# Down weights of the expert steps issued by ScalarE instead of SyncE

## The chip, the core and the metric

The kernel runs on one core of one Trainium2 chip. The metric is the device time of one execution in microseconds (us). A core has TensorE (matmuls), VectorE, ScalarE, GpSimd and SyncE, each with an instruction stream of its own, tied together by semaphores, and 16 DMA engines that all of them share.

## The reference

One layer of a decoder trunk in float32, for 1024 prompt tokens and 8 sample tokens (1032 rows of width 1024): RMSNorm, one input projection, four token mixers side by side (RWKV-7, causal pooling, a Conformer convolution, Mamba-2), gates, an output projection and a residual. Then a mixture of experts, which is the part that matters here, and a last RMSNorm:

```python
x = x + m                                    # m: the token mixers
x = x + hier_moe(rmsnorm(x, norm_ffn_g), lw) # 16 experts, hidden width 256, 2 of them for each token
...
hg = jnp.einsum('bld,edf->blef', h, moe_w_gate[e]); hu = jnp.einsum('bld,edf->blef', h, moe_w_up[e])
act = jax.nn.silu(hg) * hu * gate[..., e, None]
out = out + jnp.einsum('blef,efd->bld', act, moe_w_down[e])
```

Each token goes to one group of four experts and to the best two in it.

## The kernel before

All up to the router (about 1290 us) is not touched. The expert stage follows. The pairs of token and expert are sorted by expert and cut into slots of 32 rows that belong to one expert each. There are 80 slots, in 20 steps (`STEPS`) of four (`NS = 4`): in step i, slot j works on rows 32j to 32j+31 of the arrays with the weights of its expert, in `GU[j]` and `DN[j]`. Slot j of step i is slot 20j + i of the sorted list, so each j passes through the experts in order, and its expert mostly stays the same from one step to the next.

A table in memory, `exps`, holds for each step and slot the expert's number and a flag that says whether it differs from that of the step before. It is written once (`routed` reaches 3). The engine that issues a load reads the eight numbers of a step into registers (`look_up`), and each load has `cond=f`: with the flag at 0 nothing is moved, and the semaphore still counts up. Only the down weights of step 0 have no condition. The gate/up weights of four guessed experts (`GUESS`) are fetched before the router is through, and step 0 replaces those that were guessed wrong.

Sizes: the gate/up weights of an expert are 2 MB. They come in four pieces (`GUC = 4`, 128 rows of 4 KB, 0.5 MB each), each with its semaphore `gu_in{h}`. The down weights are 1 MB (128 rows of 8 KB), semaphore `dn_in`. Both are held once per slot number: piece h of step i+1 can be fetched only when `gu_mm{h}` says that step i has used it, and the down weights when `dn_mm0` and `dn_mm1` say so (the two halves of the output columns). Both halves read the same buffer.

TensorE's order, from line 1064:

```python
turn_rows(0); turn_rows(1); gate_up(0)
for i in range(STEPS):
    if i + 2 < STEPS: turn_rows(i + 2)      # turns the gathered rows XG, L1024
    turn_act(i)                             # L1033
    if i + 1 < STEPS: gate_up(i + 1)        # 64 matmuls, 16 for each piece, L1045
    down(i)                                 # 32 matmuls, waits for dn_in, L1059
```

`gate_up(i)` waits for the four pieces one after the other. SyncE issues all weights in one queue: for step 0 the pieces, then the down weights; then, for each i, the four pieces of step i+2, each behind its wait for `gu_mm{h}` (L473 and L475), and the down weights of step i+1 behind the waits for `dn_mm0` and `dn_mm1` (L508 to L510, issued at L486; those of step 0 at L483). ScalarE copies the turned rows (`rows_turned`, L1361), takes the Silu (`gated`, L1368) and copies the first half of the output (`downed`, L1375). VectorE multiplies (L2005), copies the turned activations (L2012) and the second half (L2018). GpSimd gathers the input rows two steps ahead (L2228, 0.5 MB a step, from a queue of its own) and scatters the output rows (L2234).

Of the kernel before, what the change touches and what calls it, by code (L numbers as in the profile page):

```python
# [13 lines left out]
P = 128  # L14
# [16 lines left out]
NE = 16  # L31
# [21 lines left out]
NS = 4  # L53
# [3 lines left out]
STEPS = (NSLOTS + NS - 1) // NS  # L57
# [85 lines left out]
def build(nc, ins, outs):  # L143
    ctx = ExitStack()
    with ctx:
# [5 lines left out]
        def sem(name):  # L151
            if name not in sems:
                sems[name] = ctx.enter_context(nc.semaphore(name))
            return sems[name]
# [41 lines left out]
        exps = ctx.enter_context(nc.sbuf_tensor("exps", [P, STEPS, 2, NS], I32))  # L196
# [172 lines left out]
        DN = [arena[:, 2 * D * j:2 * D * (j + 1)] for j in range(NS)]  # L369
# [18 lines left out]
        def _(sp):  # L388
# [70 lines left out]
            guess_gu(3)  # L459

            gu_e = ins["w_gu"].rearrange("(e p) f -> p e f", p=P)
            dn_e = ins["w_dn"].rearrange("(e p) f -> p e f", p=P)
            regs = [[ctx.enter_context(sp.register(f"slot_{s}_{q}")) for q in range(2 * NS)] for s in range(2)]

            def look_up(i):

                sp.load(regs[i % 2], exps[0:1, i:i + 1, :, :].rearrange("p a b c -> p (a b c)"))

            def load_gu(i, h):

                w = GUW // GUC
                for j in range(NS):
                    e = sp.snap(regs[i % 2][j], donate=False, min_val=0, max_val=NE - 1)  # L473
                    f = sp.snap(regs[i % 2][NS + j], donate=False, min_val=0, max_val=1)
                    sp.dma_start(GU[j][:, h * w:(h + 1) * w].unsqueeze(1), gu_e[:, bass.ds(e, 1), h * w:(h + 1) * w], cond=f  # L475
                                 ).then_inc(sem(f"gu_in{h}"), 16)

            def load_dn(i):

                for j in range(NS):  # L480
                    e = sp.snap(regs[i % 2][j], donate=False, min_val=0, max_val=NE - 1)
                    if i == 0:
                        sp.dma_start(DN[j].unsqueeze(1), dn_e[:, bass.ds(e, 1), :]).then_inc(sem("dn_in"), 16)  # L483
                    else:
                        f = sp.snap(regs[i % 2][NS + j], donate=False, min_val=0, max_val=1)
                        sp.dma_start(DN[j].unsqueeze(1), dn_e[:, bass.ds(e, 1), :], cond=f).then_inc(sem("dn_in"), 16)  # L486

            sp.wait_ge(sem("h2_out0"), 16 * 5)
            sp.wait_ge(sem("h2_out1"), 16 * 4)
            sp.wait_ge(sem("routed"), 3)  # L490
# [3 lines left out]
            sp.wait_ge(sem("xg_in0"), 16)  # L494
            for h in range(GUC):
                load_gu(0, h)
            load_dn(0)
            look_up(1)
            for h in range(GUC):
                sp.wait_ge(sem(f"gu_mm{h}"), NS)  # L500
                load_gu(1, h)
            for i in range(STEPS - 1):
                if i + 2 < STEPS:
                    look_up(i + 2)
                    for h in range(GUC):
                        sp.wait_ge(sem(f"gu_mm{h}"), NS * (i + 2))
                        load_gu(i + 2, h)
                sp.wait_ge(sem("dn_mm0"), NS * (i + 1))  # L508
                sp.wait_ge(sem("dn_mm1"), NS * (i + 1))
                load_dn(i + 1)  # L510

            sp.wait_ge(sem(f"gu_mm{GUC - 1}"), NS * STEPS)
            sp.wait_ge(sem("dn_mm1"), NS * STEPS)
# [576 lines left out]
        def _(act):  # L1090
# [42 lines left out]
            for n in range(4):  # L1133
                act.wait_ge(sem("lora_mm"), n + 1)
                dst, b = ((SG, "w0"), (AA, "a0"))[n // 2]
# [220 lines left out]
            def rows_turned(i):  # L1356

                act.wait_ge(sem("xt_mm"), i + 1)
                if i >= 2:
                    act.wait_ge(sem(f"gu_mm{GUC - 1}"), NS * (i - 1))  # L1360
                A(XT[i % 2], ps[:, 2:4, :].rearrange("p a b -> p (a b)"), ACT.Copy).then_inc(sem("xt_ev"), 1)  # L1361

            def gated(i):

                act.wait_ge(sem(f"gu_mm{GUC - 1}"), NS * (i + 1))
                if i:
                    act.wait_ge(sem("act"), i)
                A(SIL, ps[:, i % 2, 0:HID], ACT.Silu).then_inc(sem("silu"), 1)  # L1368

            def downed(i):  # L1370

                act.wait_ge(sem("dn_mm0"), NS * (i + 1))
                if i >= 2:
                    act.wait_ge(sem(f"yo_out{i % 2}"), 16 * (i // 2))
                A(YO[i % 2][:, 0:HALF], ps[:, 5, :], ACT.Copy).then_inc(sem("yo_ev0"), 1)  # L1375

            rows_turned(0)
            rows_turned(1)
            gated(0)
            for i in range(STEPS):  # L1380
                if i + 2 < STEPS:
                    rows_turned(i + 2)
                if i + 1 < STEPS:
                    gated(i + 1)
                downed(i)
            act.wait_ge(sem("xt_mm"), STEPS)
            for b, n in enumerate(ON_PE):
                for c in range(2):
# [981 lines left out]
```

## Time and profile before

| | |
|---|---|
| time before, median of 3 runs | 1639.51 us (1638.74 to 1641.35) |
| the profiled execution, its own time | 1640.04 us |
| its span, first to last instruction | 1638.2 us |
| granted TensorE clock over the span | 0.976 |
| TensorE busy with matmuls | 1523.8 us, 93% |
| expert stage, first gate/up matmul to last down matmul | about 1307.6 to 1589.7 us |

All rows below are of the profiled execution. Times at the start of a row are microseconds from the start of the span. "SPq" is SyncE issuing a DMA; "idle before <- releaser" is how long the engine stood still and what ended it. "issue" as a releaser means that the profile shows nothing that it waited for. Queue q1 is the hardware queue of SyncE, q0 that of GpSimd.

### The profile page before, as it was taken

What the parts mean: (1) busy time and instruction counts of PE and PEld (TensorE: products, weight loads), DVE (VectorE), ACT (ScalarE), POOL (GpSimd) and SP (SyncE); (2) the same over time, 40 slices, a digit from 0 to 9 for tenths busy, and PEclk for the clock granted to TensorE, in tenths of its full rate; (3) what the DMA queues carried; (4) which work ended last, traced back from release to release, by engine and by line L of the source; (5) the groups of instructions that cost most, each with busy time, mean ns of one, the idle gap of its engine ahead of it and who ended that gap; (6) DMA issues with size and microseconds to landing.
All of it is one profiled execution on the core that took longest, in us unless ns stands there. A gap on an engine that the chain in (4) does not pass through costs nothing.

```text
span 1638.2 us, 20753 instructions
## 1 busy us (share of the span) xinstructions
PE 1523.8 (93%) x8005; PEld 984.3 (60%) x8005; DVE 741.3 (45%) x1394; ACT 341.7 (21%) x633; POOL 205.6 (13%) x316
## 2 busy tenths in 40 slices
PE   8999999999999999999999999999999397978965
PEld 5888666577777777777777765666444232322312
DVE  5655199842534344636344323577844401101116
ACT  3001311412213131331313145000121211111113
POOL 3008300012111101101010010000000001101100
PEclk9999999999999999999999999999999699989997
DMA  7101011033221312111103120465200878675647
GB/s 218 52 26 52 18 40 35 30 121 102 64 71 52 111 42 73 49 56 52 48 35 125 48 106 32 174 274 180 110 39 26 292 262 327 245 263 207 224 171 301
DMA packets 47235, 194.70 MB, mean 119 GB/s; under 512 B 6408, under 2 KB 6904, under 8 KB 42400
## 3 DMA queue, kind: packets, MB, share of 16 engines
q1 hardware_dynamic: 28144, 116.13, 20.0%
q0 software_dynamic: 18992, 77.25, 13.2%
q8 instruction: 63, 1.03, 0.3%
q14 instruction: 36, 0.29, 0.1%
HBM read 353.23 MB, written 41.44 MB: 241 GB/s over the span
## 4 chain that ended last, share of the span: by engine, by line
PE 84%; DMA 6%; DVE 4%; issue 2%; SPq 2%; ACT 2%; POOL 0%; DVEq 0%; POOLq 0%; ACTq 0%
PE ps L548 29%; PE ps L616 7%; PE ps L896 7%; PE ps L945 6%; PE ps L1045 6%; PE ps L1059 3%; PE ps L840 3%; DMA arena<-in_w_gu 3%; PE ps L754 2%; PE ps L749 2%; PE ps L759 2%; PE ps L732 2%; SPq L475 1%; PE ps L563 1%; DMA scr<-h_rows,idx 1%
## 5 line engine op out<-in xcount | busy, mean ns | idle before, releaser
L548 PE MATMUL ps<-arena,wring 128*128 128x344 f32 x1728 | 528.5, 452 | 0.6 <-DVE arena L1471 0.6
L548 PEld LDWEIGHTS ps<-arena,wring 128*128 128x128 f32 x1728 | 314.4, 189 | 143.6 <-issue 1.9
L1045 PE MATMUL ps<-arena,scr 128*32 128x512 f32 x1280 | 150.4, 617 | 20.3 <-DMA arena<-in_w_gu 19.9
L2117 POOL DMA_DIRECT2D gate_scratch<-stage x96 | 52.1, 544 | 618.6 <-ACT stage L1185 542.8
L896 PE MATMUL ps<-arena,wring 128*128 128x344 f32 x384 | 111.2, 451 | 0.0
L1045 PEld LDWEIGHTS ps<-arena,scr 128*32 128x32 f32 x1280 | 39.3, 112 | 115.8 <-issue 83.7
L896 PEld LDWEIGHTS ps<-arena,wring 128*128 128x128 f32 x384 | 72.5, 189 | 38.6
L1185 ACT ACTIVATE stage<-ps 128x344 f32<-128x344 f32 x84 | 38.4, 457 | 252.8 <-PE ps L548 252.7
L2005 DVE TENSOR_TENSOR scr<-scr,ps 128x256 f32<-128x256 f32 x20 | 8.4, 421 | 181.4 <-ACT scr L1368 181.4
L1059 PE MATMUL ps<-arena,scr 128*32 128x512 f32 x640 | 76.1, 617 | 15.3 <-issue 13.9
L1702 DVE TENSOR_TENSOR scr<-scr,ps 128x512 f32<-128x512 f32 x40 | 27.5, 688 | 127.9 <-PE ps L754 127.9
L1576 DVE SCALAR_TENSOR_TENSOR arena<-arena,vec 128x1024 f32<-128x1024 f32 x60 | 74.4, 1282 | 1.1
L616 PE MATMUL ps<-scr,arena 128*128 128x258 f32 x288 | 64.3, 381 | 0.0
L840 PE MATMUL ps<-arena,wring 128*128 128x344 f32 x192 | 59.3, 470 | 3.3 <-ACT stage L1159 3.3
L1059 PEld LDWEIGHTS ps<-arena,scr 128*32 128x32 f32 x640 | 22.0, 114 | 67.0 <-issue 65.4
L616 PEld LDWEIGHTS ps<-scr,arena 128*128 128x128 f32 x288 | 54.6, 190 | 8.0
L945 PE MATMUL ps<-arena,scr 128*128 128x512 f32 x128 | 58.2, 599 | 0.0
L1471 DVE TENSOR_TENSOR arena<-arena,ps 128x258 f32<-128x258 f32 x70 | 27.9, 421 | 58.5 <-PE ps L616 58.2
L840 PEld LDWEIGHTS ps<-arena,wring 128*128 128x128 f32 x192 | 37.6, 197 | 24.6 <-ACT stage L1159 3.9
L1225 ACT ACTIVATE scr<-ps 128x512 f32<-128x512 f32 x40 | 23.9, 597 | 130.4 <-PE ps L749 130.4
L2234 POOL DMA_INDIRECT y_rows<-scr,idx x20 | 19.6, 978 | 243.7 <-DVE scr L2018 239.0
L749 PEld LDWEIGHTS ps<-scr 128*128 128x128 f32 x320 | 41.9, 191 | 8.0
(450 smaller groups left out, 2091.8 us busy)
## 6 DMA issues: line engine op xcount, KB each, us to landing
arena<-in_w_gu SPq DMA_DIRECT2D x336, 512.0 KB
arena<-in_w_dn SPq DMA_DIRECT2D x80, 1024.0 KB
wring<-in_w_all SPq DMA_DIRECT2D x55, 512.0 KB, 3.6
gate_scratch<-stage POOLq DMA_DIRECT2D x96, 172.0 KB, 2.2
arena<-gate_scratch POOLq DMA_DIRECT2D x4, 2064.0 KB, 10.5
scr<-gate_scratch POOLq DMA_DIRECT2D x4, 2064.0 KB, 10.4
arena<-y_rows SPq DMA_DIRECT2D x16, 512.0 KB, 9.6
arena<-in_w_out SPq DMA_DIRECT2D x2, 2048.0 KB, 15.7
```

Source lines behind the costliest of these rows:

```text
L548: mm = pe.matmul(ps[:, c, 0:CW], wring[:, slot, k, :], H[:, k, chunk(c)], start=k == 0, stop=k == KT - 1)
L616: mm = pe.matmul(ps[:, g % 6, 0:QT], left[k][:, j, :], src[:, j, c], start=j == 0, stop=j == 3)
L732: mm = pe.matmul(ps[:, 4 + n, (q % 2) * 256:(q % 2) * 256 + 256], (BT if n < 2 else KTB)[:, q, :], KR[:, q, :, :].rearrange("p a b -> p (a ...
L749: mm = pe.matmul(ps[:, 6, q * P:(q + 1) * P], NLB[:, q, :], U[:, q, :], start=True, stop=True)
L840: mm = pe.matmul(ps[:, 6 + m % 2, 0:CW], wring[:, n % 2, k, :], H[:, k, chunk(c)], start=k == 0, stop=k == KT - 1)
L896: mm = pe.matmul(ps[:, m % 6, 0:CW], wring[:, n % 2, 2 * b + k, :], row(2 * b + k, c * CW, (c + 1) * CW), start=k == 0, stop=k == 1)
L945: mm = pe.matmul(ps[:, bank, :], left[:, k, :], right[:, k, :], start=k == 0, stop=k == 3)
L1045: mm = pe.matmul(ps[S * j:S * (j + 1), i % 2, :], XT[i % 2][:, k * P + S * j:k * P + S * (j + 1)], GU[j][:, k * 2 * HID:(k + 1) * 2 * HID] ...
L1059: mm = pe.matmul(ps[S * j:S * (j + 1), 5 + h, :], ATB[:, k, S * j:S * (j + 1)], DN[j][:, k * D + h * HALF:k * D + (h + 1) * HALF], start=k ...
L1185: A(stage[:, c, :], ps[:, c, 0:CW], ACT.Sigmoid).then_inc(sem("evac"), 1)
L1576: ins_ = ts(dst, src, w, v("conv_b", t), MUL, ADD) if j == 0 else stt(dst, src, w, dst, MUL, ADD)
L2117: pool.dma_start(gate_scratch[:, g:g + 1, chunk(c)], stage[:, c:c + 1, :]).then_inc(sem(f"gate_out{c}"), 16)
```

## The change

The down weights of every step are issued by ScalarE. It has eight registers of its own and loads them from `exps` at each step. For step 0 it does so ahead of its first work in the stage, as soon as the table is there and the first gather has landed; for step i+1 behind the copy of the first half of step i and a wait for `dn_mm1`. SyncE keeps the pieces of gate/up and its own look-ups.

```diff
@@ SyncE
-            def load_dn(i):
-                for j in range(NS):
-                    e = sp.snap(regs[i % 2][j], ...)
-                    if i == 0:
-                        sp.dma_start(DN[j].unsqueeze(1), dn_e[:, bass.ds(e, 1), :]).then_inc(sem("dn_in"), 16)
-                    else:
-                        f = sp.snap(regs[i % 2][NS + j], ...)
-                        sp.dma_start(DN[j].unsqueeze(1), dn_e[:, bass.ds(e, 1), :], cond=f).then_inc(sem("dn_in"), 16)
...
             for h in range(GUC):
                 load_gu(0, h)
-            load_dn(0)
             look_up(1)
...
                         load_gu(i + 2, h)
-                sp.wait_ge(sem("dn_mm0"), NS * (i + 1))
-                sp.wait_ge(sem("dn_mm1"), NS * (i + 1))
-                load_dn(i + 1)
@@ ScalarE
+            regs = [ctx.enter_context(act.register(f"down_{q}")) for q in range(2 * NS)]
+            def load_dn(i):
+                act.load(regs, exps[0:1, i:i + 1, :, :].rearrange("p a b c -> p (a b c)"))
+                for j in range(NS):
...                 # the same snaps and DMAs, by act
+            act.wait_ge(sem("routed"), 3)
+            act.wait_ge(sem("xg_in0"), 16)
+            load_dn(0)
             rows_turned(0)
             rows_turned(1)
             gated(0)
             for i in range(STEPS):
                 if i + 2 < STEPS:
                     rows_turned(i + 2)
                 if i + 1 < STEPS:
                     gated(i + 1)
                 downed(i)
+                if i + 1 < STEPS:
+                    act.wait_ge(sem("dn_mm1"), NS * (i + 1))
+                    load_dn(i + 1)
```

## Rows read from the trace of the kernel before

**Rows 1.** The page, busy time of each engine and its share of the span.

```profile
PE 1523.8 (93%) x8005; PEld 984.3 (60%) x8005; DVE 741.3 (45%) x1394; ACT 341.7 (21%) x633; POOL 205.6 (13%) x316
```

**Rows 2.** Waits, 1290 to 1600: total us, times, longest.

```profile
PE ps L1045 <- DMA arena<-in_w_gu: 19.9, 9, 4.9
PE ps L1059 <- issue: 13.9, 5, 5.1
```

**Rows 3.** Timeline of TensorE: last piece of gate_up(4), and down(3).

```profile
1365.88 1.92 PE L1045 MATMUL ps<-arena,scr 128*32 128x512 f32 x16 [3.62 <-DMA arena<-in_w_gu]
1369.63 3.64 PE L1059 MATMUL ps<-arena,scr 128*32 128x512 f32 x32 [1.82 <-issue]
```

**Rows 4.** Timeline of TensorE: down(4), (9), (13), turn_rows(16), down(18).

```profile
1384.60 5.32 PE L1059 MATMUL ps<-arena,scr 128*32 128x512 f32 x32 [3.09 <-issue]
...
1460.29 5.03 PE L1059 MATMUL ps<-arena,scr 128*32 128x512 f32 x32 [5.08 <-issue]
...
1516.76 3.64 PE L1059 MATMUL ps<-arena,scr 128*32 128x512 f32 x32 [1.35 <-issue]
1520.87 1.09 PE L1024 MATMUL ps<-cst,scr 128*128 128x128 f32 x8 [0.47 <-DMA scr<-h_rows,idx]
...
1580.55 3.64 PE L1059 MATMUL ps<-arena,scr 128*32 128x512 f32 x32 [2.57 <-issue]
```

**Rows 5.** Waits of SyncE, 1250 to 1638: total us, times, longest.

```profile
SPq L509 <- PE ps L1059: 43.2, 15, 11.4
```

**Rows 6.** Timeline of SyncE's issues: gu(0), dn(0), dn(3), dn(4), gu(6), gu(11), dn(13), gu(15).

```profile
1302.89 7.85 SPq L475 DMA_DIRECT2D arena<-in_w_gu  x16
...
1310.95 1.98 SPq L483 DMA_DIRECT2D arena<-in_w_dn  x4
...
1356.04 1.56 SPq L486 DMA_DIRECT2D arena<-in_w_dn  x4
...
1373.70 1.78 SPq L486 DMA_DIRECT2D arena<-in_w_dn  x4
1376.77 8.20 SPq L475 DMA_DIRECT2D arena<-in_w_gu  x16
...
1450.47 6.84 SPq L475 DMA_DIRECT2D arena<-in_w_gu  x16
...
1507.63 1.79 SPq L486 DMA_DIRECT2D arena<-in_w_dn  x4
1510.67 8.14 SPq L475 DMA_DIRECT2D arena<-in_w_gu  x16
```

**Rows 7.** Lines L467 (register loads) and L475: ns min/median/max.

```profile
L467 SPq TENSOR_LOAD <-exps x20: 361/524/727, 1289.9 to 1558.9; - x20
...
L475 SPq DMA_DIRECT2D arena<-in_w_gu x320: 2/73/352, 1302.9 to 1569.0; - x160
```

**Rows 8.** DMA queues, 1433 to 1435: packets, MB, share of 16 engines.

```profile
q1 hardware_dynamic: 116, 0.42, 51.5%
q0 software_dynamic: 117, 0.41, 50.6%
```

**Rows 9.** DMA queues, 1454 to 1457, q1 with down weights.

```profile
q1 hardware_dynamic: 115, 0.81, 64.4%
q0 software_dynamic: 116, 0.47, 38.1%
```

**Rows 10.** Timeline of TensorE: gate_up(0), matmuls and one of their weight loads.

```profile
1312.60 7.05 PE L1045 MATMUL ps<-arena,scr 128*32 128x512 f32 x48 [2.12 <-DMA arena<-in_w_gu]
1317.33 0.13 PEld L1045 LDWEIGHTS ps<-arena,scr 128*32 128x32 f32 x4 [0.30 <-DMA arena<-in_w_gu]
```

**Rows 11.** Timeline of GpSimd: the gather of step 3.

```profile
1307.93 0.94 POOL L2228 DMA_INDIRECT scr<-h_rows,idx  x1 [1.73 <-PE ps L1024]
```

**Rows 12.** Busy time in 1384.5 to 1388: engines, then granted clock, DMA share, GB/s.

```profile
1384.50:1388.00 3.50, 3.40 (x17) 1.00 (x21) 0.00 (x0) 0.00 (x0) 0.00 (x0) 0.52 1.03 418
```

More of the change, by code:

```diff
@@ L461, in _ @@
             gu_e = ins["w_gu"].rearrange("(e p) f -> p e f", p=P)
-            dn_e = ins["w_dn"].rearrange("(e p) f -> p e f", p=P)
             regs = [[ctx.enter_context(sp.register(f"slot_{s}_{q}")) for q in range(2 * NS)] for s in range(2)]
@@ L476, in load_gu @@
                                  ).then_inc(sem(f"gu_in{h}"), 16)
-            def load_dn(i):
-                for j in range(NS):
-                    e = sp.snap(regs[i % 2][j], donate=False, min_val=0, max_val=NE - 1)
-                    if i == 0:
-                        sp.dma_start(DN[j].unsqueeze(1), dn_e[:, bass.ds(e, 1), :]).then_inc(sem("dn_in"), 16)
-                    else:
-                        f = sp.snap(regs[i % 2][NS + j], donate=False, min_val=0, max_val=1)
-                        sp.dma_start(DN[j].unsqueeze(1), dn_e[:, bass.ds(e, 1), :], cond=f).then_inc(sem("dn_in"), 16)
             sp.wait_ge(sem("h2_out0"), 16 * 5)
@@ L1375, in downed @@
                 A(YO[i % 2][:, 0:HALF], ps[:, 5, :], ACT.Copy).then_inc(sem("yo_ev0"), 1)
+            dn_e = ins["w_dn"].rearrange("(e p) f -> p e f", p=P)
+            regs = [ctx.enter_context(act.register(f"down_{q}")) for q in range(2 * NS)]
+            def load_dn(i):
+                act.load(regs, exps[0:1, i:i + 1, :, :].rearrange("p a b c -> p (a b c)"))
+                for j in range(NS):
+                    e = act.snap(regs[j], donate=False, min_val=0, max_val=NE - 1)
+                    if i == 0:
+                        act.dma_start(DN[j].unsqueeze(1), dn_e[:, bass.ds(e, 1), :]).then_inc(sem("dn_in"), 16)
+                    else:
+                        f = act.snap(regs[NS + j], donate=False, min_val=0, max_val=1)
+                        act.dma_start(DN[j].unsqueeze(1), dn_e[:, bass.ds(e, 1), :], cond=f).then_inc(sem("dn_in"), 16)
+            act.wait_ge(sem("routed"), 3)
+            act.wait_ge(sem("xg_in0"), 16)
+            load_dn(0)
             rows_turned(0)
```

## The prediction

> **What bounds the kernel now.** I read the page first: TensorE is busy for 93% of the span [rows 1], so only its idle time can be won or made. Then the waits of the expert stage (about 1303 to 1590 us). TensorE is stopped there in two ways: 19.9 us before gate/up matmuls until a piece of weights lands, and 13.9 us before down matmuls, five times, which the profile calls "issue" [rows 2]. In those five places nothing but `dn_in` is missing, so I read them as waits for down weights. Next, where they are: gate_up(4) stops 3.62 us for its last piece, then down(3) 1.82 us [rows 3]; down(4), down(9), down(13) and down(18) stop 3.09, 5.08, 1.35 and 2.57 us [rows 4]. The other steps show no stop of this kind.
>
> Is SyncE what is late? It sat 43.2 us waiting for TensorE's down matmuls [rows 5], and its order follows TensorE's: the pieces of step i+2 go out during gate_up(i+1), the down weights of step i+1 after down(i), and the next piece can be issued only when gate_up(i+2) has used its buffer. The first piece goes out 2 to 3 us after the last down issue (1373.70 + 1.78 to 1376.77, 1507.63 + 1.79 to 1510.67) [rows 6]. So a down issue holds up no later piece that could have gone. What is short in the stalls is transfer time. A transfer whose expert stays the same is skipped; its issue takes 0.073 us, one that runs 0.34 [rows 7].
>
> **The look-up and issue on ScalarE.** Removed from SyncE: four issues a step. Added to ScalarE: a register load (0.524 us median on SyncE) [rows 7] and the same four issues, 1.2 to 2.0 us [rows 6]. ScalarE comes here after the copy of the first half of down(i) and waits for the second half, which TensorE ends about when it did for SyncE. The look-up now stands behind that wait, so each down transfer starts some 0.5 us later. Behind it on ScalarE stands the copy of the turned rows (needed a step later) and the Silu (due after a 7 us gate_up). In the steady step they hide the 2.5 to 3 us. The 0.5 us shows only where down already waits for its weights: down(4), (9), (13), (18): 4 x 0.5 = +2.0. Bounds: 0, if the register load is fetched faster than SyncE's, to +3.2 at 0.8 each.
>
> **What two hardware queues do to the order.** Until now down weights of step i+1 stand in one queue behind the pieces of step i+2 that TensorE needs first, and ahead of those of step i+3. From now on they are in a queue of their own. The trace has a second queue already, POOL's gathers and scatters, and shows how two queues share. Where both carry 4 KB rows they moved 116 and 117 packets, 0.42 and 0.41 MB [rows 8]. Where the hardware queue carries down weights (8 KB rows), it was 115 and 116 packets, but 0.81 against 0.47 MB, in 3 us: 427 GB/s, with shares that add up to all 16 engines [rows 9]. So queues take turns by packet, and a down transfer gets two bytes for each byte of gate/up. At 427 GB/s an engine needs 0.154 us for 4 KB and 0.307 for 8 KB. A transfer is 128 rows, 8 for each engine. A turn is thus 0.46 us with down and one other queue busy, and 0.61 with all three.
>
> The Trainium skill (DMA: Bandwidth & Descriptors, Issuing engines are not separate DMA queues) says that transfers issued by different engines run on the same 16 DMA engines and interleave, so that only the sequencer's issue time is saved. The trace agrees with the first half: 0.81 and 0.47 MB in 3 us out of a full set of engines [rows 9].
>
> **Step 0, dn(0) against gu(0).** Before, dn(0), 4 MB, was issued at 1310.95, after all pieces of gu(0) (1302.89 to 1310.7) [rows 6]. One of the four guessed experts is reloaded, so each piece is one transfer of 0.5 MB; the first goes out at about 1303.7 and moves from about 1304.8 (estimates from the row). gate_up(0) ran its last 48 matmuls from 1312.60, the last piece landed at 1317.33, and it ended at 1319.65 [rows 10]. Now ScalarE issues dn(0) from about 1303.2, as soon as the first gather lands, and its 32 rows per engine are there with the first piece. Piece 0: 8 turns of 0.46 = 3.7 us, to 1308.5. POOL's gathers (2) and (3), 16 rows an engine, come in from about 1308 [rows 11]. Pieces 1 and 2: 8 turns of 0.61 = 4.9 us each, to 1318.3; the gathers are then done. Piece 3: 3.7 us, to 1322.0, plus about 1.2 us to the semaphore (estimate from dn(9), whose full engines end a little before down(9) starts): 1323.2. Its 16 matmuls take 1.92 [rows 3]: gate_up(0) ends at 1325.1 instead of 1319.65. **+5.5.** dn(0) is landed long before down(0) then, which wins nothing, since down(0) did not stop before. Lower bound: if the queues shared bytes evenly, the pieces would land some 2 us late, +1.9. Upper bound: the matmuls run at the low clock after these idle stretches, +7.5. ScalarE also turns XT(0) some 1 us later, which lies under the wait for piece 1 (2.12 us) [rows 10]. I take 5.5, as the packet counts say.
>
> **dn(3) against gu(4).** dn(3), one expert, was issued at 1356.04 [rows 6] behind pieces of gu(4) that were still moving. Now it passes them. The same bytes are moved by the same time, when dn(3) landed (1369.6), but the last to land is piece 3 of gu(4), not dn(3). Behind it still lie 1.92 us of matmuls: down(3) starts at 1371.5 instead of 1369.63 [rows 3]. **+1.9.** Below: 0, if piece 3 kept its turn; it can't be a gain over 1.8, the wait itself. The idle stretch before piece 3 grows from 3.6 to 4.9 us. After the 3.09 us before down(4) the granted clock was 0.52 [rows 12] (the 1.2 GHz level) and the product took 5.32 instead of 3.64 [rows 4, 3]. After 3.62 us in gate_up(4) it had not fallen. For 4.9 us I count such a fall: **+1.7** (0 to 1.7).
>
> **dn(4) against gu(6), dn(13) against gu(15).** dn(4), two experts, was issued at 1373.70 and gu(6) behind it at 1376.77; dn(13) at 1507.63 and gu(15) at 1510.67 [rows 6]. Each had SyncE's queue to itself until it was through. Now a third queue takes turns from some 2 us after the first down row. dn(4) then has about 10 of its 16 rows per engine left; with POOL also busy each costs 0.61 instead of 0.46: 8 to 10 x 0.15 = 1.2 to 1.5, and about two of them share with gate/up alone at 0.46 instead of 0.31: +0.3. **+1.7 for down(4), +1.5 for down(13)**, whose last rows met POOL's later. Its wait is followed by one of 0.47 for a gather [rows 4], which the shift takes in: -0.4. Bounds: 0 to 2.5 each. dn(9) and dn(18) have no gate/up transfers beside them (gu(11) is all skipped, 16 issues in 6.84 us [rows 6], and there is no step 20): only the 0.5 us.
>
> **Sum.** 2.0 + 5.5 + 1.9 + 1.7 + 1.7 + 1.5 - 0.4 = 13.9 us. The stops of gate_up(9), (13) and (18) stay, as dn(8), dn(12) and dn(17) are skipped. Nothing takes the sum back: steps 5 to 8, 10 to 12 and 14 to 17 are bound by TensorE and are only shifted. The profiled execution took 1640.0 (span 1638.2): 1653.9, which is 1653.4 against the median of 1639.5, since that lies 0.5 below.
>
> **The rivals.**
> 1. The forecast, 1653.4, chance 0.48.
> 2. The clock falls in every new idle stretch: also in gate_up(0) (+1.9), before down(13), whose stop grows from 1.35 to over 3 us (+1.7), and down(18), 2.57 to 3.1 us (+1.7). For it speaks down(4) with 3.09 us [rows 4], against it gate_up(4) with 3.62 at full clock [rows 3]. 1639.5 + 13.9 + 5.3 = 1658.7. Chance 0.17.
> 3. The hardware queues share bytes evenly, or a piece passes between large rows: 1.9 for step 0, 1.9 for dn(3), 1.0 for each of dn(4) and dn(13), 2.0 for the look-up, no clock: +7.8 - 0.4, 1646.9. Against it stand the packet counts of [rows 9], but these are of POOL's queue, not of a second hardware one. Chance 0.20.
> 4. Nothing measurable: SyncE's small pieces find their turn at once, and only look-ups show: +2.0, 1641.5. Chance 0.08. This needs spare engines, and in the stalls they are full.
> 5. Faster, by one mechanism: the stops before down come from standing behind gate/up in one queue. With its own, dn(3) lands some 5 us sooner and the 1.82 us are gone; dn(4) is issued sooner too, and if the engines gave both queues more together, its 3.09 would shrink. At -1.8 - 3.1 it gives 1634.6. It decides once passing costs piece 3 of gu(4) less than 1.8 us; the full engines speak against it. Chance 0.04.
>
> **How the numbers follow.** A measurement of this kernel tells 0.2%, 3.3 us, from no change. The range takes in cases 1 and 3 and most of 2: 1644.5 to 1661; what is left out are 4, 5 and a little of 2 and 3, under 2 in 10. Rivals 1 to 3 are slower by over 0.2% (0.85, less a little of 3), rival 4 and that little make "same" 0.10, rival 5 faster 0.04; the 0.03 left goes to slower, for costs that I have not seen. Slower 0.86, same 0.10, faster 0.04.
>
> **What would show it.** In the profile after: gate_up(0)'s last piece lands at about 1323 and the matmuls of L1045 wait several times in step 0; down(3) follows gate_up(4) without a stop, and gate_up(4) stops over 6 us; the stops before down(4) and down(13) are 2 us longer; those before down(9) and down(18) 0.5. In the waits, the total of L1045 for its weights rises from 19.9 to about 28, that of L1059 from 13.9 to about 17. If gate_up(0) ends before 1321.6, the sharing by packets is wrong; if down(3) starts before 1369.6, passing costs nothing. A wait of TensorE for ScalarE anywhere (for a copy of turned rows that stands behind the new issues) would be a cost that I have at zero.

## The result, and the profile after

The changed kernel takes 1659.6 us, median of 5 (1657.1 to 1661.6), against 1641.0 us (1638.7 to 1641.5) for the kernel before on the same chip: ratio 1.0112, interval 1.0093 to 1.0130, +18.6 us. I had forecast 1653.4, range 1644.5 to 1661: the sign held, the size was 6 us short. The change cost 18.6 us where my sum had 13.9; the rest is that the kernel before has a median of 1641.0 here and had 1639.5 in its first three runs.

In the changed kernel L474 is SyncE's gate/up issue, L1371 and L1374 ScalarE's down issues, L1367 its look-up, L1030 the matmuls of gate_up, L1044 those of down (L1045 and L1059 before), L1009 and L1346 the turning of rows and ScalarE's copy of them. First the page: TensorE's busy time, then each hardware queue, then the down issues.

```profile
PE 1531.1 (92%) x8005; PEld 986.9 (60%) x8005; DVE 741.2 (45%) x1394; ACT 341.6 (21%) x633; POOL 205.6 (12%) x316
...
q1 hardware_dynamic: 25552, 97.25, 17.0%
q10 hardware_dynamic: 2592, 18.88, 3.2%
...
arena<-in_w_dn ACTq DMA_DIRECT2D x80, 1024.0 KB
```

TensorE runs the same 8005 matmuls, but 7.3 us longer than in [rows 1]: some of them run at a lower clock. q10 is ScalarE's new queue, with all of the down weights. Now the waits of the expert stage (total us, times, longest).

```profile
PE ps L1030 <- DMA arena<-in_w_gu: 24.1, 12, 5.3
...
PE ps L1044 <- issue: 19.6, 5, 6.9
...
PE ps L1009 <- ACT scr L1346: 6.0, 1, 6.0
```

and in the kernel before, the line that answers to the third:

```profile
PE ps L1024 <- ACT scr L1361: 1.2, 1, 1.2
```

The first two answer to [rows 2]: +4.2 and +5.7 us. The five stops ahead of down are not the same five: that of down(3) is gone, and one ahead of down(19) has come. The third has grown by 4.8 us: TensorE waits once for ScalarE's copy. The timeline of ScalarE and then of TensorE shows where:

```profile
1306.96 5.51 ACTq L1371 DMA_DIRECT2D arena<-in_w_dn  x4
1312.52 1.02 ACT L1346 ACTIVATE scr<-ps 128x1024 f32<-128x1024 f32 x1 [26.16 <-issue]
```

```profile
1313.68 1.94 PE L1009 MATMUL ps<-cst,scr 128*128 128x128 f32 x8 [5.97 <-ACT scr L1346]
1315.56 5.51 PE L1030 MATMUL ps<-arena,scr 128*32 128x512 f32 x32
1323.46 1.92 PE L1030 MATMUL ps<-arena,scr 128*32 128x512 f32 x16 [2.39 <-DMA arena<-in_w_gu]
1327.92 1.92 PE L1030 MATMUL ps<-arena,scr 128*32 128x512 f32 x16 [2.54 <-DMA arena<-in_w_gu]
...
1370.37 1.92 PE L1030 MATMUL ps<-arena,scr 128*32 128x512 f32 x16 [0.45 <-DMA arena<-in_w_gu]
1377.58 3.50 PE L1030 MATMUL ps<-arena,scr 128*32 128x512 f32 x16 [5.29 <-DMA arena<-in_w_gu]
1380.91 3.61 PE L1044 MATMUL ps<-arena,scr 128*32 128x512 f32 x32
...
1397.76 5.34 PE L1044 MATMUL ps<-arena,scr 128*32 128x512 f32 x32 [5.00 <-issue]
...
1475.51 5.75 PE L1044 MATMUL ps<-arena,scr 128*32 128x512 f32 x32 [6.93 <-issue]
...
1534.50 5.26 PE L1044 MATMUL ps<-arena,scr 128*32 128x512 f32 x32 [2.93 <-issue]
...
1598.79 5.34 PE L1044 MATMUL ps<-arena,scr 128*32 128x512 f32 x32 [2.89 <-issue]
```

The first block is step 0: the turning of the second rows waits 5.97 us (1.21 before) while ScalarE issues dn(0), and then gate_up(0) still stops twice for pieces. The second is gate_up(4) and down(3): the old 1.82 us ahead of down(3) [rows 3] are gone, and the last 16 matmuls of gate_up(4) took 3.50 instead of 1.92. The last four are down(4), (9), (13) and (18), to be held against [rows 4].

To place the rest, I count from the first gather of the stage, because what lies ahead of it is untouched by the edit and differed by 3.2 us between the two profiles (1298.22 and 1301.45; in a second profile of the kernel before it was 1299.83, and over all fourteen profiles of this document it lies between 1298.2 and 1303.4, with kernels in which ScalarE issues down weights at both ends). This is how late the changed kernel is, against the kernel before, at the end of each down product:

| end of | before | after | late by |
|---|---|---|---|
| down(0) | 33.4 | 40.3 | 6.9 |
| down(3) | 75.1 | 83.1 | 8.0 |
| down(4) | 91.7 | 101.6 | 9.9 |
| down(9) | 167.1 | 179.8 | 12.7 |
| down(13) | 222.2 | 238.3 | 16.1 |
| down(18) | 286.0 | 302.7 | 16.7 |
| down(19) | 291.4 | 308.6 | 17.2 |

So step 0 costs 6.9, the passing of gu(4) 1.1, and 8.7 lies at the four stops: these are 5.6 us longer and the products behind them 4.1, of which about 1 us is made up, most of it in gate_up(18). By my sum it had been 5.5, 3.6 and 4.8. The last 0.5 us comes at down(19), which stops longer than in the kernel before (the second line):

```profile
1606.38 3.64 PE L1044 MATMUL ps<-arena,scr 128*32 128x512 f32 x32 [1.88 <-issue]
```

```profile
1585.94 3.64 PE L1059 MATMUL ps<-arena,scr 128*32 128x512 f32 x32 [1.38 <-DVE scr L2012]
```

Nothing is moved for step 19, but its semaphore counts up only with the four skipped issues, and the last of them ends 0.06 us ahead of down(19) here and 0.07 before, where the profile names VectorE. They too stand behind the late look-up; my sum had this at nothing.

The queues in 1320 to 1323 (packets, MB, share of 16 engines), with all three at work:

```profile
q10 hardware_dynamic: 88, 0.61, 48.5%
q0 software_dynamic: 79, 0.32, 26.2%
q1 hardware_dynamic: 83, 0.32, 25.9%
```

Near-equal packets and nearly twice the bytes for the 8 KB rows: turns by packet hold for a second hardware queue as for GpSimd's in [rows 9]. The Trainium skill (DMA: Bandwidth & Descriptors, Queues, rings and completion order) says that an engine goes round its queues at the boundaries of packets. A packet there is a group, some 9 to 17 descriptors as a rule; a packet of these rows is one row of weights. The trace agrees that the turns are even (88, 79 and 83); how many rows make one turn these counts do not show.

### The profile page after: what moved, and what is told of

Read it like the earlier page. It is cut to its first block, busy times and chain, and to the rows that moved or that the text cites. A ratio compares the mean times of both kernels' runs of the same rounds, so it can differ in the third digit from the quotient of the medians.

```text
span 1658.2 us, 20757 instructions
## 1 busy us (share of the span) xinstructions
PE 1531.1 (92%) x8005; PEld 986.9 (60%) x8005; DVE 741.2 (45%) x1394; ACT 341.6 (21%) x633; POOL 205.6 (12%) x316
## 4 chain that ended last, share of the span: by engine, by line
PE 84%; DMA 6%; DVE 4%; issue 3%; SPq 2%; ACT 2%; POOL 0%; DVEq 0%; POOLq 0%; ACTq 0%
PE ps L533 29%; PE ps L601 7%; PE ps L881 7%; PE ps L930 6%; PE ps L1030 6%; PE ps L1044 4%; DMA arena<-in_w_gu 4%; PE ps L825 3%; PE ps L734 2%; PE ps L739 2%; PE ps L717 2%; PE ps L744 2%; SPq L474 1%; PE ps L548 1%; PE ps L1009 1%
## 5 line engine op out<-in xcount | busy, mean ns | idle before, releaser
L1030 PE MATMUL ps<-arena,scr 128*32 128x512 f32 x1280 | 150.7, 617 | 24.2 <-DMA arena<-in_w_gu 24.1
L1030 PEld LDWEIGHTS ps<-arena,scr 128*32 128x32 f32 x1280 | 39.1, 112 | 119.9 <-issue 82.2
L1044 PE MATMUL ps<-arena,scr 128*32 128x512 f32 x640 | 80.6, 648 | 19.6 <-issue 19.6
L1044 PEld LDWEIGHTS ps<-arena,scr 128*32 128x32 f32 x640 | 22.9, 119 | 75.2 <-issue 75.2
L2239 POOL DMA_INDIRECT y_rows<-scr,idx x20 | 19.6, 979 | 256.1 <-DVE scr L2023 250.9
L2023 DVE COPY scr<-ps 128x512 f32<-128x512 f32 x20 | 13.8, 692 | 80.8 <-PE ps L1044 80.8
```

The source lines that it names most:

```text
L1030: mm = pe.matmul(ps[S * j:S * (j + 1), i % 2, :], XT[i % 2][:, k * P + S * j:k * P + S * (j + 1)], GU[j][:, k * 2 * HID:(k + 1) * 2 * HID] ...
L1044: mm = pe.matmul(ps[S * j:S * (j + 1), 5 + h, :], ATB[:, k, S * j:S * (j + 1)], DN[j][:, k * D + h * HALF:k * D + (h + 1) * HALF], start=k ...
```

## The experiments

Ratios are against the kernel before on the same chip; us are the ratio times 1640. "Stops" are those ahead of down(4), (9), (13), (18) in the profile; "down(0)" and "down(19)" are their ends after the first gather, and "profiled" is the profiled execution's time less the median of its kernel, in us.

| kernel | ratio (interval) | us | profiled | down(0) | stops | sum | down(19) |
|---|---|---|---|---|---|---|---|
| before | | | | 33.4 | 3.1, 5.1, 1.3, 2.6 | 12.1 | 291.4 |
| before, again | 0.9999 (0.9984 to 1.0014) | 0 | -0.8 | 32.8 | 2.9, 4.7, 1.3, 2.2 | 11.1 | 289.5 |
| changed kernel | 1.0112 (1.0093 to 1.0130) | +18.4 | +0.4 | 40.3 | 5.0, 6.9, 2.9, 2.9 | 17.7 | 308.6 |
| dn(0) on SyncE | 1.0062 (1.0045 to 1.0079) | +10.2 | -2.0 | 32.8 | 5.6, 6.0, 2.9, 3.5 | 17.9 | 295.7 |
| only dn(0) moved | 1.0057 (1.0035 to 1.0078) | +9.3 | -5.1 | 40.0 | 2.8, 5.5, 1.4, 2.4 | 12.0 | 292.6 |
| early small DMA | 1.0139 (1.0114 to 1.0164) | +22.8 | +1.2 | 42.1 | 5.4, 6.9, 3.6, 2.9 | 18.7 | 312.5 |
| dn(0) after the turns | 1.0066 (1.0046 to 1.0087) | +10.8 | +0.4 | 34.1 | 5.3, 7.3, 2.8, 3.1 | 18.6 | 299.7 |
| look-up ahead | 1.0059 (1.0037 to 1.0081) | +9.7 | +1.6 | 40.3 | 3.1, 5.5, 1.7, 2.2 | 12.5 | 301.3 |
| gate/up behind down | 1.0124 (1.0101 to 1.0146) | +20.3 | -1.1 | 40.0 | 4.2, 5.6, 2.4, 2.9 | 15.1 | 306.2 |
| before, in halves | 0.9998 (0.9984 to 1.0012) | 0 | +4.1 | 33.5 | 0, 0.9, 0, 0 | 0.9 | 292.6 |
| late look-up on SyncE | 1.0034 (1.0020 to 1.0048) | +5.6 | -3.8 | 32.9 | 4.5, 6.1, 2.3, 3.0 | 16.0 | 293.1 |
| both repairs | 1.0047 (1.0030 to 1.0064) | +7.7 | -7.9 | 37.1 | 3.4, 5.1, 1.8, 2.2 | 12.5 | 291.0 |
| both, down held back | 1.0076 (1.0053 to 1.0099) | +12.5 | -6.7 | 37.2 | 3.5, 6.8, 1.6, 2.3 | 14.3 | 298.0 |
| both, in halves | 1.0033 (1.0020 to 1.0046) | +5.4 | +0.3 | 36.0 | 0.7 at one of them | 0.7 | 298.0 |

"Profiled" matters for the reading. The executions of one kernel differ by up to 13 us, and the profile is of one of them. Where its number is far below zero, the profile shows less than the price that the ratio tells. A difference between the ratios of two kernels is good to some 0.003, or 4 to 5 us.

**The kernel before once more.** No edit: how far two profiles of one kernel differ.

> The kernel before, unchanged, as a control. Its ratio to itself is 1.000 within 0.15%. The changed kernel's first gather starts at 1301.5 us of its span, the profile of before has it at 1298.2; theory (the part ahead of the expert stage isn't touched, the 3 us are what executions differ by): this profile's first gather lies anywhere from 1298 to 1302. Rival (the added instructions shift what comes ahead): 1298.2 again, within 0.5. The stops before down(3), (4), (9), (13), (18) are within 0.7 us of 1.8, 3.1, 5.1, 1.4 and 2.6.

Its four stops sum to 11.1 (12.1 before) and its waits for gate/up to 18.5 (20.3). A difference of 1 us in such a sum says little. gate_up(4)'s last piece began its work 8.4 us after the step's start here and 9.8 there.

**Step 0 alone, from both sides.** dn(0) back on SyncE, or nothing but dn(0) moved:

```diff
 # dn(0) on SyncE: in SyncE's program, behind the pieces of gu(0)
+            for j in range(NS):
+                e = sp.snap(regs[0][j], donate=False, min_val=0, max_val=NE - 1)
+                sp.dma_start(DN[j].unsqueeze(1), dn_e[:, bass.ds(e, 1), :]).then_inc(sem("dn_in"), 16)
 # and in ScalarE's
-            act.wait_ge(sem("xg_in0"), 16)
-            load_dn(0)
```

> The changed kernel with one part undone: the down weights of step 0 go out on SyncE again, behind gu(0); steps 1 to 19 stay on ScalarE. In the changed kernel down(0) ended 6.9 us later than before, counted from the first gather, and down(19) 17.2 later. Theory (step 0 is a cost by itself, and delays add up): 7 us come back, 1652.6 us, slower than before by 11 to 12; gate_up(0) ends about 21.4 us after the first gather. Rival (a loss of step 0 would have been absorbed by later stops, and the later steps cost it all): less than 3 us come back, 1657 or more. Second rival (ScalarE's first DMA pays a start of its own wherever it stands): step 3, which then has the first one, gets 3 to 5 us longer and only 2 to 4 come back.

> The kernel before with the down weights of step 0 alone issued by ScalarE, ahead of its first copy; all other steps on SyncE. Theory: +7.0 us, 1648.0, all of it ahead of down(0), and from there the steps of the kernel before, with the stops before down(3), (4), (9), (13), (18) at 1.8, 3.1, 5.1, 1.4 and 2.6 us. Rival (the loss of step 0 is absorbed later): under +3. Sum with the run that puts step 0 back: the two differences to before should add up to that of the changed kernel, 18.6, if the parts are independent.

Back on SyncE gives +10.2, only dn(0) +9.3; together 19.5, where the change costs 18.4. By the times the two parts add up. In the first kernel down(0) ends as before (32.8) and the stops are as long as in the changed kernel; in the second it is the other way round (40.0, 12.0). The price of step 0 in the profile is 6.6 to 6.9, or 7.2 to 7.5 against the 32.8 of the control; in the times it is 8.2 and 9.3, each good to some 4. Whether a later step takes part of it back is not settled by the profile: the one of the second kernel is of an execution 5 us faster than the median, and of the 6.6 us late at down(0) only 1.2 are left at down(19). The rival of under +3 falls by the interval (+5.7 to +12.8). In the first kernel the first issue of ScalarE that moves anything, in step 3, took 0.36 us, so the second rival of that run falls too.

**Is it ScalarE's hold, or the sharing?** In the changed kernel the first down issue took 2.95 us of the 5.51; the others were 0.35 to 0.94. Two kernels take the hold away. One puts a small DMA, which nothing reads, on ScalarE's queue long before; the other issues dn(0) behind both copies of turned rows:

```diff
 # early small DMA, ahead of ScalarE's wait for the router
+            act.dma_start(warm[:, :], ins["vec"][:, 0:16]).then_inc(sem("vec_in"), 16)
...
 # dn(0) after the turns
-            load_dn(0)
             rows_turned(0)
             rows_turned(1)
+            load_dn(0)
```

> The changed kernel with one small DMA (128 rows of 64 bytes, read by nothing) issued by ScalarE some 27 us ahead, while it waits for the router. In the changed kernel ScalarE's first issue took 2.95 us against 0.34, and its first packet moved 6.1 us after the issue against 1.0 in later steps. Theory (a start cost of the first DMA on ScalarE's queue): the first issue of dn(0) takes about 0.35 us and moves after 1.0; ScalarE is free 2.6 us sooner, gate_up(0) starts that much sooner, but dn(0) then shares with gu(0) from the start, so the last piece still lands at about 25 us after the first gather and only 1 to 2 us come back: 1658. Rival (SyncE's issues going on at the same time slow ScalarE's): the first issue stays at 3 us and nothing comes back, 1659.6.

> The changed kernel with the down weights of step 0 issued by ScalarE behind its copies of the turned rows of steps 0 and 1, instead of ahead of them. It takes away the hold on ScalarE (turn_rows(1) waited 5.97 us for its copy, gate_up(0) began 4.7 us later) and leaves the sharing. Theory (the hold costs more than the sharing in step 0): gate_up(0) begins at 9.4 us after the first gather and its last piece lands at about 21 to 22 instead of 26.5, 4 to 5 us come back: 1655. Rival (the queues' sharing is the whole cost, the hold is hidden under it): the last piece lands at 25 or later, under 1.5 us come back.

With the early DMA the timeline of ScalarE and of TensorE reads:

```profile
1307.31 2.04 ACTq L1373 DMA_DIRECT2D arena<-in_w_dn  x4
```

```profile
1312.96 3.64 PE L1031 MATMUL ps<-arena,scr 128*32 128x512 f32 x16 [0.45 <-DMA arena<-in_w_gu]
1319.36 2.98 PE L1031 MATMUL ps<-arena,scr 128*32 128x512 f32 x16 [2.75 <-DMA arena<-in_w_gu]
1325.63 6.09 PE L1031 MATMUL ps<-arena,scr 128*32 128x512 f32 x32 [3.29 <-DMA arena<-in_w_gu]
```

The hold is down from 5.51 to 2.04, gate_up(0) starts 2.7 us sooner after the first gather (11.4 against 14.1), and ends 1.8 later (30.2 against 28.4): the down rows start sooner too (first packet 2.3 us after the issue against 6.1) and take turns with more of the pieces. I had expected 1 to 2 us back; the measured time is 4.4 us above that of the changed kernel, which the intervals don't quite set apart from no difference. Taking the hold away alone wins nothing. Issued after the turns:

```profile
1315.69 3.64 PE L1030 MATMUL ps<-arena,scr 128*32 128x512 f32 x32 [1.29 <-DMA arena<-in_w_gu]
1319.68 1.92 PE L1030 MATMUL ps<-arena,scr 128*32 128x512 f32 x16 [0.35 <-DMA arena<-in_w_gu]
```

The last matmuls of gate_up(0) start 18.0 us after the first gather, 8.5 sooner than in the changed kernel, and down(0) ends at 34.1. This kernel takes away both, since its first down packet comes 16.6 us after the first gather, about when the last of gu(0) has moved. What is left at step 0 is +0.8 (+1.4 against the control), and down(0) now waits 2.10 us for dn(0); against the changed kernel it gains 7.6 us in the measured time.

**The late look-up.** I had it at 0.5 us for each of four stops. Here it is taken away, and alone brought into the old order:

```diff
 # look-up ahead, ScalarE: the register load moves ahead of the wait
+                    look(i + 1)
                     act.wait_ge(sem("dn_mm1"), NS * (i + 1))
                     load_dn(i + 1)
...
 # late look-up on SyncE: the kernel before with one line more
                 sp.wait_ge(sem("dn_mm1"), NS * (i + 1))
+                look_up(i + 1)
                 load_dn(i + 1)
```

> The changed kernel with ScalarE's register load of each step ahead of its wait for dn_mm1 instead of behind it. Theory (the load, 0.55 us on ScalarE, delays each down transfer by that much, which shows where down waits for it): the stops before down(4), (9), (13) and (18) are 0.5 us shorter than 5.0, 6.9, 2.9 and 2.9, and 2.0 us come back: 1657.6. Rival (it is the order in the queues alone): no more than 0.5 us comes back, and the stops stay.

> The kernel before, all weights on SyncE, but SyncE loads the registers of step i+1 once more behind its waits for the down product, ahead of the down issues: the issue comes about 0.55 us later, in the old queue and the old order. Before and its control stop 11 to 12 us in all before down(4), (9), (13), (18), the kernels with a late look-up on ScalarE 17.7 to 18.8, the one with the look-up ahead 12.5. Theory (half a microsecond of lateness is what lengthens these stops, since it moves bytes from the time when the engines are free to that when they share with POOL's; the queue has no part): the four stops come to 15 to 18 us and the time to +4 to +6, 1645. Rival (it is the third queue's turns): they stay under 14, +1 to +2.

TensorE's down(4), (9), (13), (18) with the look-up ahead, all else as in the changed kernel:

```profile
1398.54 5.25 PE L1044 MATMUL ps<-arena,scr 128*32 128x512 f32 x32 [3.09 <-issue]
...
1474.72 6.40 PE L1044 MATMUL ps<-arena,scr 128*32 128x512 f32 x32 [5.52 <-issue]
...
1530.81 3.64 PE L1044 MATMUL ps<-arena,scr 128*32 128x512 f32 x32 [1.70 <-issue]
...
1592.55 5.34 PE L1044 MATMUL ps<-arena,scr 128*32 128x512 f32 x32 [2.19 <-issue]
```

These are nearly the stops of [rows 4] again (12.5 against 12.1 us), although the down weights still stand in a queue of their own and share with gu(6) and gu(15): up to the last packet of dn(4), SyncE's queue moved 0.34 MB beside it. The measured gain over the changed kernel is 8.7 us, good to some 5, where I expected 2. And with the late look-up as the only edit of the kernel before:

```profile
1384.94 5.91 PE L1060 MATMUL ps<-arena,scr 128*32 128x512 f32 x32 [4.53 <-issue]
...
1460.95 5.45 PE L1060 MATMUL ps<-arena,scr 128*32 128x512 f32 x32 [6.11 <-issue]
...
1515.35 5.34 PE L1060 MATMUL ps<-arena,scr 128*32 128x512 f32 x32 [2.32 <-issue]
...
1579.47 5.34 PE L1060 MATMUL ps<-arena,scr 128*32 128x512 f32 x32 [3.05 <-issue]
```

The stops grow by 3.9 us (4.9 against the kernel's second profile), down(13) and (18) need 5.34 instead of 3.64, and the kernel takes 5.6 us more, as the theory of this run had it. A register load of some 0.55 us on the path of a stop thus costs 1.0 to 1.2 us in the mean of the four (0.5 to 1.7 at one of them), and the clock on top. In this profile, of an execution 3.8 us faster than the median, shorter waits for pieces (16.4 against 19.9 us) hide most of it: down(19) ends only 1.7 us late (3.6 against the control).

Why more than itself? The issue comes 0.99 us after the end of down(3) instead of 0.43, but then the transfer takes longer too. From the issue of dn(4) to its last packet it is 10.2 us before, 11.1 with the late look-up on SyncE, 10.1 with the look-up ahead and 11.4 in the changed kernel. In that time GpSimd's queue moved 0.66, 0.97, 0.50 and 0.89 MB: its first packet comes 5.7 us after the issue of dn(4) before and 5.4 with the late look-up, so a later down transfer meets more of the gather. The 0.31 MB more of the first pair are 0.7 us at 427 GB/s (estimate from [rows 9]). At down(18) the transfer is not longer (8.9 before, 8.8 and 8.7 with a late look-up), and the stop grew by 0.3 to 0.5, no more than the delay.

**Does gate/up sharing lengthen the stops?** Here SyncE waits until the down weights of step i+1 have landed before it sends the pieces of step i+3, so that nothing of gate/up shares with dn(4) and dn(13):

```diff
 # SyncE, behind look_up(i + 2)
+                sp.wait_ge(sem("dn_in"), 16 * NS * (i + 1))
```

> The changed kernel, in which SyncE waits, ahead of the pieces of step i+2, until the down weights of step i have landed. It puts back one half of the old order: pieces don't move beside a down transfer that is needed before them. Theory (taking turns by packet with gu(6) and gu(15) costs down(4) and down(13) about 1.5 us each): their stops fall from 5.0 and 2.9 to 3.5 and 1.5 us, 3 us come back, with the clock's part in down(13) up to 4.5: 1655 to 1656.6. Rival (the stops grew by the later issue and by POOL's transfers): both stay within 0.5 us, and gate_up(6) and gate_up(15), whose pieces go out later, begin to wait: 1659.6 or more.

The waits of this kernel, to be read against the first two of the changed kernel's:

```profile
PE ps L1031 <- DMA arena<-in_w_gu: 24.3, 14, 5.3
PE ps L1045 <- issue: 16.9, 5, 5.6
```

The stops ahead of down lose 2.6 us, but the kernel is no faster (1.0124, and 1.0112 for the changed one): gate_up(6) now stops 1.3 us and gate_up(15) 0.4, where they had not. The rival expected these. Of the 2.6 us only 0.8 at down(4) and 0.5 at down(13) lie where the sharing went; 1.3 lie at down(9), which shared nothing with gate/up, so a part is scatter. But the late look-up on SyncE, which doesn't share either, says the same: the two kernels have 4.2 and 4.5 us at down(4), 2.4 and 2.3 at down(13), and the four with both a late look-up and sharing 5.0 to 5.6 and 2.8 to 3.6. So behind a late look-up the sharing costs some 0.5 to 1 us at each.

**In halves.** The down weights go out as two halves along the rows, the first as soon as its buffer half is read, and down runs half by half:

```diff
+            def load_dn(i, k):
...
+                    dst, src = DN[j][:, k * D:(k + 1) * D].unsqueeze(1), dn_e[:, bass.ds(e, 1), k * D:(k + 1) * D]
...
 # SyncE's loop
                 sp.wait_ge(sem("dn_mm0"), NS * (i + 1))
+                load_dn(i + 1, 0)
                 sp.wait_ge(sem("dn_mm1"), NS * (i + 1))
-                load_dn(i + 1)
+                load_dn(i + 1, 1)
```

> The kernel before, all weights on SyncE, with the down product turned inside out: k is the outer loop, both banks are filled in each half, and the down weights come in two transfers of 4 KB rows, one for each k, each with a semaphore of its own and each issued when its half of the buffer is free. Theory (the stops before down are transfer time that begins only when down(i-1) has ended and has to end before down(i) begins): the first half goes out 1.7 us sooner and only it is waited for, the second lands under 16 matmuls; the five stops, 13.9 us, fall to under 5 and the time to about 1631, 0.5% faster than before. Rival (SyncE's four more issues a step, 0.4 us each, and the later first bank eat it): 1637 to 1641.

```profile
PE ps L1048 <- DMA arena<-in_w_gu: 24.1, 15, 4.0
PE ps L1062 <- DMA arena<-in_w_dn: 7.5, 2, 4.3
PE ps L1062 <- issue: 0.9, 1, 0.9
```

The stops ahead of down are gone (13.9 to 0.9), and the time is that of the kernel before (0.9998), where I had expected 1631; the profiled execution is 4 us slower than the median. Part of them came back inside down (7.5), part in gate_up (24.1 against 19.9), and down(4) and (9) then took 8.6 and 9.9 us with these gaps and the clock. An idle stretch that is bound by the bytes moves when its order is changed; it doesn't go.

**Both repairs, and two things on top.** Look-up ahead and dn(0) after the turns; then this with the down issue held until the pieces of the step after have landed; then this in halves, issued by ScalarE:

```diff
 # both, down held back
                     act.wait_ge(sem("dn_mm1"), NS * (i + 1))
+                    if i + 2 < STEPS:
+                        act.wait_ge(sem(f"gu_in{GUC - 1}"), 16 * NS * (i + 4))
                     load_dn(i + 1)
```

> The changed kernel with both repairs: the look-up ahead of the wait, and the down weights of step 0 behind the copies of the turned rows of steps 0 and 1. Alone they brought back 8.5 and 7.5 us of the 18.6. Theory (they are independent, and nothing but the passing of gu(4) by dn(3) is left): 1640 to 1644, at most 2 to 3 us over before. Rival (both shortened the same later stops, so that they don't add up): 1647 or more.

> The kernel with both repairs, in which ScalarE also waits, ahead of the down issues of step i+1, until the last piece of gate/up of step i+2 has landed: down weights no longer pass pieces that are needed first. Theory (in gate_up(4) dn(3) makes the last piece some 2 us later): that piece starts 9 us after gate_up(4) began instead of 10.5 to 12, but dn(3) then starts only when it has landed, and down(3) stops 3 to 4 us: 1 to 3 us slower than with both repairs alone. Rival (order costs nothing, only bytes count): the same within 1 us.

> The kernel with both repairs, with the down product turned inside out and its weights in two halves of 4 KB rows, each issued by ScalarE as soon as its half of the buffer is free, ahead of its copy of the output. On SyncE these halves took the stops before down from 12 to 1 us and gave them back in gate_up and in the middle of down. Theory (the bursts are bound by the engines' 427 GB/s, whoever issues): no gain either, 1639 to 1644. Rival (on SyncE the four more issues a step made the pieces late; ScalarE has time for them): 1632 to 1636, faster than before.

Both repairs leave +7.7 us, where the two gains of 7.6 and 8.7 would have left 2; the gap of 5.6 is not clear of the noise of the four kernels that it is taken from. The profile can't place it, since it is of the fastest of six executions, 7.9 us below the median, and its down(19) ends 0.4 us sooner than before. What it does show is that step 0 is back at +3.8: its first issue was a short one (0.40 us; 4.87 with dn(0) after the turns alone), the first down packet came 13.2 us after the first gather instead of 16.6, and so dn(0) meets the pieces of gu(0) again. The repair of step 0 had rested on that long issue. This can be a part of the +7.7, and is not shown to be all of it. gate_up(4) and down(3) with both repairs, and then with down held back:

```profile
1371.85 3.61 PE L1030 MATMUL ps<-arena,scr 128*32 128x512 f32 x16 [5.24 <-DMA arena<-in_w_gu]
1375.21 3.69 PE L1044 MATMUL ps<-arena,scr 128*32 128x512 f32 x32
```

```profile
1368.02 1.92 PE L1030 MATMUL ps<-arena,scr 128*32 128x512 f32 x16 [1.71 <-DMA arena<-in_w_gu]
...
1376.66 3.64 PE L1044 MATMUL ps<-arena,scr 128*32 128x512 f32 x16 [6.71 <-issue]
```

Held back, the piece's matmuls begin 3.4 us sooner after the step's start (7.7 against 11.1) and run at full speed, and the stop ahead of down(3) comes back as 6.71 us. In these two profiles down(3) ends 4.3 us later for it; the time is 4.8 us longer (+12.5 against +7.7), just at the edge of the noise. The piece's lateness is the down weights' passing; what the old order did better, I take it, was to send them right behind the last piece. In halves +5.4 us are left, more than I had expected (1639 to 1644). The stops ahead of down have turned into others here, most of all into waits for the gathered rows (the second line; before they were 6.4 us in two places):

```profile
PE ps L1030 <- DMA arena<-in_w_gu: 20.9, 11, 4.7
PE ps L1009 <- DMA scr<-h_rows,idx: 17.6, 7, 5.9
PE ps L1044 <- DMA arena<-in_w_dn: 4.0, 1, 4.0
```

Nothing with down on ScalarE comes down to the kernel before, so there is no version to put forward.

## Why the prediction was right, and where its sizes were off

**The late look-up, +2.0 predicted.** This is the term that was mis-sized, and it carries most of what I missed. Measured alone it is +5.6, and taken away 8.7 come back. The stops sum to 17.7 instead of 12.1, at down(13) and (18) the product took 5.3 instead of 3.64, and a fifth place, down(19), was not in the sum (+0.5). My step "each down transfer starts some 0.5 us later" was right, its price of 0.5 per stop was not: the stop grew by about twice the delay in the mean. For dn(4) the bytes show why: the transfer gives up time in which the engines had nothing else, and ends in time shared with gathers. That the clock then fell in two more products is seen, and why it did is not shown.

**The clock.** The forecast had it fall in gate_up(4) only, rival 2 in three more places. After 5.29 us it fell there (16 matmuls 3.50, 1.92 before). It also fell at down(13) and down(18), as rival 2 had it; in gate_up(0) the last two pieces ran at full speed (1.92 each), only its first 32 matmuls, behind the wait for ScalarE, did not (5.51). That fall was not a new one: the kernel before had it in the same place, 2.83 for the first 16 and 7.05 for the other 48 [rows 10], 9.9 us in all against 9.4 after. I had overlooked it; rival 2 had it as +1.9. Busy time, then granted clock, DMA share and GB/s, at the end of gate_up(4), in down(4), (9), (13) and (18):

```profile
1375.00:1381.00 6.00, 3.42 (x20) 0.88 (x24) 0.00 (x0) 0.00 (x0) 0.00 (x0) 0.72 0.89 363
...
1397.50:1403.50 6.00, 5.74 (x36) 2.07 (x37) 0.28 (x1) 0.60 (x1) 0.00 (x0) 0.72 0.59 242
1475.50:1481.50 6.00, 5.99 (x35) 1.75 (x36) 0.11 (x1) 0.60 (x1) 0.00 (x0) 0.64 0.00 0
1534.50:1540.00 5.50, 5.50 (x35) 1.59 (x36) 0.09 (x1) 0.60 (x1) 0.00 (x0) 0.70 0.93 373
1598.80:1604.00 5.20, 5.20 (x32) 1.52 (x32) 0.00 (x0) 0.60 (x1) 0.00 (x0) 0.67 0.00 0
```

A mean of about 0.7 is a stretch with a part at each of the two levels, 1.2 and 2.4 GHz: in down(4) the granted clock was 0.50 in 1399 to 1401 and 0.93 in 1401 to 1403, in down(18) still 1.00 in 1598.8 to 1599.2 and 0.50 in 1599.8 to 1602. The last two rows are new: 32 matmuls at full clock took 3.64 there before [rows 4].

**Step 0, +5.5 predicted, 6.9 in the profile.** The sharing is there: queues in turns, and an end of gate_up(0) 7.0 us later (28.4 against 21.4). But what I had at zero, ScalarE's hold, made TensorE's wait for its copy 5.97 us instead of 1.21, and gate_up(0) began 4.7 us later; dn(0) too started later, and less of it shared. The two stand in for each other: without the hold the sharing takes its place (30.2), without both only 0.8 is left. That 5.5 came so near to 6.9 is luck. The sum was near; its working held for the case without a hold, where it was too low by about 3.

**dn(3) past gu(4), +3.6 predicted, +1.1 in the profile.** Each step of it was seen: down(3) without a stop, gate_up(4)'s last piece later, the clock down. The size is where I was off. The last piece began its matmuls 9.8 us after the start of gate_up(4) before, 11.3 after: 1.5 later, where I had 3.7. (My own numbers did not agree here: a piece that is 3.7 us later makes the idle stretch 7.3 us, and I wrote 4.9.) With the slower matmuls (3.50 - 1.92 = 1.6) that is 3.1, less the 1.8 of the stop that went. Over kernels it scatters: 8.0 to 9.8 in four profiles with the old order, mean 8.7; 9.9 to 12.3 in seven in which dn(3) passes, mean 11.1. So 2.4 in the mean. "The same bytes are moved by the same time" made the piece the last to land, and it wasn't quite; what landed behind it I have not traced. My mark of "over 6 us" for the stops of gate_up(4) was missed (5.29 + 0.45 = 5.74).

**Sharing with gu(6) and gu(15), +3.2 less 0.4.** This was smaller. With the look-up ahead and this sharing in place, down(4) stops 3.1 to 3.4 and down(13) 1.7 to 1.8 us, where three profiles with the old order have 2.8 to 3.1 and 1.3 to 1.4: 0.3 to 0.4 each. Behind the late look-up it is some 0.5 to 1 each. The marks that I had set, down(4) and (13) 2 us longer, were met (+1.9, +1.6), but down(9), which shares nothing and was to grow by 0.5, grew by 1.9: most of it is the look-up. That the forecast total came near rests partly on this error being of the size of the one in the look-up, and that is luck. So it is with the two totals: the waits for gate/up came to 24.1 us (28 forecast), those ahead of down to 19.6 (17).

**The sum.** 6.9 + 1.1 + 8.7 + 0.5 = 17.2 in the stage, and 3.2 ahead of it, less 0.4 behind it, make the 20.0 us by which the profiled executions differ (1659.98 and 1640.04). The 3.2 are not explained: the control showed 1.6 of it with no edit at all, and both repairs and the one with down held back, which also have the down weights on ScalarE, 0.9 and 0.3. By medians it is 18.6.

The rivals: even sharing (3) falls with the packet counts; only look-ups (4) has more truth in its +5.6 than I gave it, but not the whole; faster (5) was seen as to down(3) and lost the 1.82 us again in gate_up(4).

## What to carry to other kernels

A transfer moved to an engine's queue of its own no longer stands behind what is needed sooner: it passes it, with bytes in the ratio of the row sizes, so ask which of the two TensorE needs first. A short serial instruction ahead of an issue whose transfer ends a stop should be costed at more than its own length, and taken off the path; here that one line cost 5.6 us as the only edit, and taking it away brought back 8.7 of 18. Where stops are bound by bytes, a new order only moves them: in all four kernels that tried one the stops came back elsewhere.

## What the runs showed of the hardware that I had not expected

- The first down issue on ScalarE's queue took 2.95 us, and all four 5.51, with 4.40 and 6.79 in two other kernels; with an earlier small DMA on the queue it was 2.04 for all four. But with both repairs, and no such DMA, the four took 2.22. The first one took 2.42 to 4.87 us in the five kernels without such a DMA in which ScalarE loaded the registers of step 0 right ahead of it, and 0.40 to 0.41 in the three in which its copies of the turned rows stood between. What makes it long stays open.
- The first packet came 6.1 us after the issue at step 0, and about 1.0 us after that of dn(9), where the engines were quiet, on either queue.
- 0.55 us of lateness gave 1.0 to 1.2 us of stop in the mean of four, 0.5 to 1.7 at one of them, and a fall of the clock in two products that had run at full speed.
- down(18) ran at the lower level after a stop of 2.19 us with the look-up ahead, and at full clock after 2.57 us before [rows 4]: the length of the stop alone doesn't decide. In both, 64 matmuls without a break stood ahead of the stop and the granted clock was 1.00 up to its end; behind it it was 0.62 and 0.53 in one, and 1.00 in the other.
